# Latent attention in three-pass fp32 on one core: positional queries projected for two heads at once, and stage-opening weights split one stage earlier

## The reference

```python
def mla_layer(x, norm_g, w_in, q_norm, w_uq, w_out, k_nope, k_rope, v, cos, sin):
    h = rms_norm(x, norm_g)
    u = h @ w_in
    c_q = rms_norm(u[..., :Q_RANK], q_norm)          # 384 latents
    gate = u[..., Q_RANK:]                           # 8 heads x 128
    q = jnp.einsum("bsc,chd->bshd", c_q, w_uq)       # 128 + 64 per head
    q_nope = q[..., :QK_NOPE]
    q_rope = apply_rope(q[..., QK_NOPE:], cos[None, :, None], sin[None, :, None])
    o = causal_block_attention(q_nope, q_rope, k_nope, k_rope, v)
    y = o.reshape(bsz, seq, N_HEADS * V_DIM) * jax.nn.silu(gate)
    return y @ w_out
```

## Time and profile before

| what | value |
|---|---|
| median of 3 runs | 2606.91 us (2606.51 to 2610.33) |
| profiled execution | 2605.84 us |
| its span | 2604.0 us |
| mean granted TensorE clock | 0.980 |
| latent heads, 600 to 870 us | PE busy 263.3 of 270 us, DVE 150.9, ACT 121.5 |

### The profile page before, as it was taken

The page is one execution under the profiler, slowest core; times in us unless marked ns, Lnnn a source line. Parts: engine busy times, 40 slices in busy tenths (PEclk is TensorE's granted clock), DMA queues, the critical chain, the costliest instruction groups (busy, mean ns, idle before and its releaser), DMA issues. The chain is left out here.

```text
span 2604.0 us, 32719 instructions
## 1 busy us (share of the span) xinstructions
PE 2470.3 (95%) x12285; PEld 2046.1 (79%) x12285; DVE 1605.4 (62%) x2886; ACT 1197.0 (46%) x2167; POOL 191.5 (7%) x114
## 2 busy tenths in 40 slices
PE   7999899989999999899999999999899998999987
PEld 5777687877888777788888888888678786888876
DVE  6676766335655547666666666652666665888874
ACT  4554533224444444455555654432445434555542
POOL 0000021000000043000000000000122120000012
PEclk9999999999999999999999999999899999999998
DMA  3222321222221331111111011233344421111133
GB/s 132 81 75 87 126 89 57 73 88 82 65 92 55 114 109 57 41 41 41 34 41 41 26 40 41 97 129 139 130 153 144 132 81 37 41 32 48 49 118 113
DMA packets 89688, 206.56 MB, mean 79 GB/s; under 512 B 7120, under 2 KB 39760, under 8 KB 88528
## 3 DMA queue, kind: packets, MB, share of 16 engines
q1 hardware_dynamic: 89552, 204.72, 24.0%
HBM read 163.73 MB, written 40.96 MB: 79 GB/s over the span
## 5 line engine op out<-in xcount | busy, mean ns | idle before, releaser
L197 PE MATMUL acc<-operand_hi,w_hi 128*128 128x512 f32 x1878 | 762.0, 406 | 44.1 <-DVE w_lo L192 19.9
L199 PE MATMUL acc<-operand_hi,w_lo 128*128 128x512 f32 x1878 | 740.4, 394 | 0.0
L198 PE MATMUL acc<-operand_lo,w_hi 128*128 128x512 f32 x1878 | 739.5, 394 | 0.0
L197 PEld LDWEIGHTS acc<-operand_hi,w_hi 128*128 128x128 f32 x1878 | 357.3, 190 | 124.4 <-DVE w_lo L192 22.0
L199 PEld LDWEIGHTS acc<-operand_hi,w_lo 128*128 128x128 f32 x1878 | 356.5, 190 | 77.8
L198 PEld LDWEIGHTS acc<-operand_lo,w_hi 128*128 128x128 f32 x1878 | 357.4, 190 | 71.2 <-issue 3.6
L192 DVE TENSOR_TENSOR w_lo<-w_raw,w_hi 128x1024 fp32r<-128x1024 f32 (+1 forms) x209 | 234.6, 1123 | 187.1 <-ACT w_hi L186 185.4
L186 ACT ACTIVATE w_hi<-w_raw 128x1024 fp32r<-128x1024 f32 (+1 forms) x209 | 202.4, 969 | 287.0 <-PE aux L199 155.4
L197 PE MATMUL aux<-operand_hi,w_hi 128*128 128x512 f32 x602 | 246.8, 410 | 23.8 <-DVE w_lo L192 9.0
L199 PE MATMUL aux<-operand_hi,w_lo 128*128 128x512 f32 x602 | 237.9, 395 | 0.0
L198 PE MATMUL aux<-operand_lo,w_hi 128*128 128x512 f32 x602 | 237.8, 395 | 0.0
(11 more groups left out here) (424 smaller groups left out, 4175.6 us busy)
## 6 DMA issues: line engine op xcount, KB each, us to landing
w_raw<-in_stream SPq DMA_DIRECT2D x209, 512.0 KB, 3.6
ssd_e<-cs_scratch SPq DMA_DIRECT2D x8, 1024.0 KB, 7.3
g_scratch<-ssd_work SPq DMA_DIRECT2D x12, 512.0 KB, 2.9
ssd_xbc<-g_scratch SPq DMA_DIRECT2D x8, 768.0 KB, 5.5
y_scratch<-rnn_y SPq DMA_DIRECT2D x10, 512.0 KB, 2.6
out_a_raw<-y_scratch SPq DMA_DIRECT2D x20, 256.0 KB, 4.3
resid<-in_x SPq DMA_DIRECT2D x8, 512.0 KB, 8.4
g_scratch<-mlai_g SPq DMA_DIRECT2D x8, 512.0 KB, 2.9
```

The costliest lines, as they stand in the source:

```text
L197: pe.matmul(out, w_hi, x_hi, start=first, stop=False)
L198: pe.matmul(out, w_hi, x_lo, start=False, stop=False)
L199: return pe.matmul(out, w_lo, x_hi, start=False, stop=last)
```

## The change

1. The r tile now carries the 64 columns of two heads (b and b + 1, b even) side by side, without the swapped copy. It is loaded by two DMAs of 64-column pieces (`load_positional`). Odd heads have no r unit; a list `tiles` gives the order. ACT copies the product to SBUF (`evacuate("r")`), and DVE rotates a head in four operations, one step apart; for even heads b the next head is rotated at t = 1 to 4, for odd ones at t = 2 to 5, in front of the maximum except the first. `rope_low` moves to t = 6, behind `lower("k")`; ACT's `rotated` to t = 5. In odd heads q moves to t = 4.
2. Tile 2 of `out_b` and `out_sw` is split in step 7 of the last head or pair (`begun.split = 1`). The third tile of the layers behind `out_b` and `out_ssd` is split at the end of the projection in front, ahead of `final(1)`; `out_a` had that already.
3. `lag` = 2 for all: the second of the two tiles at the end runs two chunks behind the first.
4. For tile 0 of a projection DVE adds the residual behind the split.
5. In `mla_inputs` the third tile uses another PSUM bank; the second-last gate tile begins alone for three chunks; the v tile of head 0 is split to 256 columns only; the loads of tiles 2 and 3 of the heads are issued ahead of the last store of a gate.
6. The window attention takes the values out ahead of the keys.

```diff
 def project_halves(...):
+    skip = begun.split if begun is not None else 0
...
-        lag = 2 if after == "latent" else 0
+        lag = 2
...
-            if q + 2 < tiles + ahead:
+            if skip <= q and q + 2 < tiles + ahead:
...
+        if after != "end":
             split_hi(act, k, tile(tiles + 2))
...
-            dve.tensor_tensor(resid(q), total(q), resid(q), ALU.add).then_inc(k.acc_free[t.slot], 1)
-            if q + 2 < tiles + ahead:
+            if q and q + 2 < tiles + ahead:
+                dve.tensor_tensor(resid(q), total(q), resid(q), ALU.add).then_inc(k.acc_free[t.slot], 1)
+            if skip <= q and q + 2 < tiles + ahead:
                 split_lo(dve, k, tile(q + 2))
                 if extra and q + 2 < tiles:
                     piece_low(dve, q + 2)
+            if not q or q + 2 >= tiles + ahead:
+                dve.tensor_tensor(resid(q), total(q), resid(q), ALU.add).then_inc(k.acc_free[t.slot], 1)
...
-        if after == "latent":
+        if after != "end":
             split_lo(dve, k, tile(tiles + 2))
 def mla_inputs(...):
-        return k.acc[:, tile(h).slot, :]
+        return k.aux[:, 0, :] if h == 2 else k.acc[:, tile(h).slot, :]
...
-        store(count - 1)
...
+        front = 3
+        wait_tile(pe, k, tile(count - 2))
+        for n in range(front):
+            part(count - 2, n)
+        wait_tile(pe, k, tile(count - 1))
+        for n in range(front):
+            part(count - 1, n)
+        for n in range(front, DT):
+            for h in (count - 2, count - 1):
+                part(h, n)
...
-                split_lo(dve, k, tile(h + 2))
+                split_lo(dve, k, tile(h + 2), (KV_KT if h + 2 == count else DT) * P)
...
+def load_positional(sp, k, t, row):
+    sp.wait_ge(k.w_lo[t.slot], t.before)
+    for n, done in ((0, k.positional), (1, k.w_loaded[t.slot])):
+        sp.dma_start(k.w_raw[:, t.slot, 0:Q_KT * P].rearrange("p (t c) -> p t c", c=P)[:, :, HD * n:HD * n + HD],
+                     k.stream[row + 4 * n].rearrange("p (t c) -> p t c", c=P)[:, 0:Q_KT, 0:HD]).then_inc(done, 16)
 def mla_heads(...):
+    tiles = [(name, b) for b in range(MLA_HEADS) for name in (MLA_ORDER if b % 2 == 0 else "vqk")]
...
         for n in range(2, 4):
             load(n)
+        store_last(sp)
...
-                if t == 2 and more:
+                if t == 2 and more and b % 2:
                     units("r", b + 1)
-                if t == 3 and more:
+                if t == 3 + b % 2 and more:
                     units("q", b + 1)
...
+            if part < 2:
+                to, of = (at + 32 * m for m in (part, 1 - part))
+                dve.tensor_tensor(turned[to:to + 32, :], raw[of:of + 32, :], rope[64 + 32 * part:96 + 32 * part, :],
+                                  ALU.mult).then_inc(s["ra"], 1)
+            elif part == 2:
+                dve.wait_ge(s["ra"], 3 * b + 2)
+                dve.tensor_tensor(raw[at:at + 64, :], raw[at:at + 64, :], rope[0:64, :], ALU.mult).then_inc(s["ra"], 1)
+            else:
+                dve.wait_ge(s["ra"], 3 * b + 3)
+                dve.tensor_tensor(turned[at:at + 64, :], turned[at:at + 64, :], raw[at:at + 64, :], ALU.add
+                                  ).then_inc(s["rb"], 1)
...
-                        rotate(b + 1)
                         split("k", b + 1)
+                    if (3 <= t <= 5 and odd) or (1 <= t <= 4 and not odd):
+                        rotate(b + 1, t - 1 - odd)
                     if t == 6:
                         lower("k", b + 1)
+                        rope_low(b + 1)
...
+                    if t == 2 and odd:
+                        rotate(b + 1, 0)
-                        rope_low(b + 1)
 def window_attention(...):
+        t = Tile(j0, 1, per, 0)
+        act.wait_ge(k.tile_done[t.slot], t.before + 1)
+        act.activation(vt[:, :], k.acc[:, t.slot, :], ACT.Identity, bias=bv).then_inc(k.acc_free[t.slot], 1)
         t = Tile(j0, 0, per, 0)
...
+                    if n == 7:
+                        split_lo(dve, k, begun.tile(2))
```

More of the change, by code:

```diff
@@ L1275, in _ @@
         for h in range(2, count - 2):
-            wait_tile(pe, k, tile(h))
+            if h == 2:
+                pe.wait_ge(k.w_lo[tile(h).slot], tile(h).before + 1)
+            else:
+                wait_tile(pe, k, tile(h))
             multiply(pe, k, tile(h), acc(h), DT).then_inc(k.tile_done[tile(h).slot], 1)
@@ L1287, in _, with part @@
                 stats_pe_spread(pe, k, s, 1, k.aux[:, 1, :])
[L1288 to L1300, removed]
-                mm.then_inc(s["free"], 1)
+        def part(h, n):
+            t, w = tile(h), slice(order[n] * P, (order[n] + 1) * P)
+            for b in range(2):
+                mm = three_passes(pe, bank(acc(h), b), k.w_hi_sb[:, t.slot, w], k.w_lo_sb[:, t.slot, w],
+                                  bank(k.xh[:, order[n], :], b), bank(k.xl[:, order[n], :], b), n == 0, n == DT - 1)
+            if n == DT - 1:
+                mm.then_inc(k.tile_done[t.slot], 1)
+            if n < len(places) and h == count - 1:
+                mm.then_inc(s["free"], 1)
+        front = 3
[8 more added lines that the diff above has]
+                part(h, n)
     @block.gpsimd
@@ L1426, in mla_heads @@
     y = g
[L1427 removed]
+    t12 = sb("t12", [P, 2, S])
     v = sb("v", [P, S])
@@ L1478, in _ @@
             if b < last:
-                for n in range(4 * b + 6, 4 * b + 10):
+                for n in range(start(b + 1) + 2, start(b + 2) + 2):
                     load(n)
@@ L1629, in split @@
         def split(name, b):
+            if name == "r" and b < MLA_HEADS:
+                act.wait_ge(k.positional, 8 * b + 16)
             split_hi(act, k, tile(name, b), width(name, b))
@@ L1638, in evacuate @@
                 act.activation(kh[par], proj("k", b), ACT.Copy).then_inc(s["kh"], 1)
+            elif name == "r":
+                if b:
+                    act.wait_ge(s["rb"], b)
+                act.activation(t12[:, 1, :], proj("r", b), ACT.Copy).then_inc(k.acc_free[t.slot], 1)
             else:
@@ L1654, in _ @@
         evacuate("v", 0)
-        act.wait_ge(k.tile_done[tile("r", 0).slot], tile("r", 0).before + 1)
+        evacuate("r", 0)
         split("k", 0)
@@ L1684, in _ @@
                                    ACT.Copy).then_inc(s["pth"], 1)
+                if not more and t == 7:
+                    act.wait_ge(k.tile_done[begun.tile(0).slot], begun.tile(0).before + 1)
+                    split_hi(act, k, begun.tile(2))
                 if t == 0:
@@ L1698, in _ @@
                         evacuate("k", b + 1)
-                        split("r", b + 2)
+                        split("q" if odd else "r", b + 2)
                     if t == 7:
@@ L1758, in _ @@
         split("k", 0)
-        rotate(0)
+        for part in range(4):
+            rotate(0, part)
         lower("q", 0)
@@ L1763, in _ @@
         lower("k", 0)
-        split("r", 1)
+        split("q", 1)
         maximum(0, 0)
@@ L3181, in _ @@
                                bias=bk[rows(e), :]).then_inc(s[name], 1)
-        split_hi(act, k, Tile(j0, 2, per, 0))
         act_slopes(act, 0, 0)
-        t = Tile(j0, 1, per, 0)
-        act.wait_ge(k.tile_done[t.slot], t.before + 1)
-        act.activation(vt[:, :], k.acc[:, t.slot, :], ACT.Identity, bias=bv).then_inc(k.acc_free[t.slot], 1)
         split_hi(act, k, Tile(j0, 3, per, 0))
```

83 lines of the change are left out of this document (51 added, 32 removed).

## The result

The changed kernel took a median of 2594.43 us (2592.61 to 2595.43, four runs), the kernel before, beside it, 2608.36 us; the ratio is 0.995, 95% interval 0.9938 to 0.9963, so 9.7 to 16.2 us less. The profiled execution took 2594.74 us, 11.1 us less than that of before. Faster, as forecast, and within 2 us of the predicted 2592.7. The gain that was forecast is 14.2 us; the medians give 13.9, the two profiled executions 11.1.

A forecast was written before the change was run, and what follows sets the result against it. The prediction took PE, busy 95% of the span, as the bound nearly everywhere. Its terms summed to -14.2 us, which from the median of 2606.9 us gave 2592.7 us, with a range of 2580 to 2602 us.

The forecast's parts named there:

- four r units: Heads 1, 3, 5 and 7 lose their positional unit of 18 matmuls, 4.10 us each: -16.4 us.
- low queries behind keys: At seven changes of head, one more DVE operation ahead of the output makes PE wait 1.2 us more: +8.4 us.
- gate pair: Last two gate tiles, near 546 us: PE's 3.9 us gap and 2.4 us of half clock go, -6.3 us.
- opening of head 0: Narrow v split and earlier q load shorten the chain to the first score: -2.9 us, bounds 0 and -5.
- barrier at 428: PE no longer waits for ACT's copy out of the bank, since the new bank is free: -1.1 us.
- end of `out_b`: The split ahead of DVE's scalings delays ACT and PE at the barrier: +2.9 us; good-side bound -3.0.
- `out_ssd` and window start: Values turned earlier, but PE's next tile waits for the keys' bank; with clock and residual, +1.6 us.
- positional loads: Loads of 64 columns, in 256-byte pieces, have some 20 us before use: 0 us.
- rival D: Clock falls within the heads, 11 stretches of 2.4 us: 2619 us, slower than before; chance 0.04.
- B: Rival: new waits at head changes and the end of `out_b` don't come: 2581.4 us; chance 0.2.
- C: Rival: DVE becomes the bound in heads without an r unit, up to 8 us: 2600.7 us; chance 0.17.
- E: Rival: shared r tile is late or saves nothing, 16.4 us given back: 2609 us, no change; chance 0.04.

The follow-up runs named there:

- run 1: Changed kernel with the low part of the next head's queries moved to step 5, behind the maximum: 2580.72 us, ratio 0.9897.
- run 5: Changed kernel with the last two gate tiles beginning together again: 2593.5 us, ratio 0.9957.
- run 8: Kernel before with only the change's parts on the heads, the opening of head 0 and the bank at 428: 2597.27 us, ratio 0.9968.
- run 7: Changed kernel with tile 0's residual added ahead of the split again in `out_a` and `out_ssd`: one run, 2597.1 us.
- 9: Changed kernel with run 1's and run 7's edits, `out_b` scalings ahead of the split, first window query tile in a free bank: 2568.75 us, ratio 0.9853.
- 10: The version of run 9 without the lag of two chunks behind the differential attention and state-space stage: 2570.81 us, ratio 0.9853.

## Why the prediction was right, point by point

| step | predicted | measured | from |
|---|---|---|---|
| four r units | -16.4 | -19.0 | heads, before against run 1 |
| low queries behind keys | +8.4 | +12.3 | heads, after against run 1 |
| gate pair | -6.3 | -6.4 (3.9 pause, 2.5 clock) | profiles before and after; -5.5 in run 5 |
| opening of head 0 | -2.9 | -3.1 | 1.4 ahead of v, 1.7 up to the score |
| barrier at 428 | -1.1 | -1.1 | table |
| starts of `out_b`, `out_sw` | -0.7 | -1.2 | table |
| end of `out_b` | +2.9 | +2.2 pause, +2.5 inside | table |
| `out_ssd` and window start | +1.6 | +3.3, not shown to be the change | table; run 8 has it too |
| `out_a` | +0.3 | not to be told from 0 | run 7 |
| positional loads | 0 | 0 | below |

**The sum was better than its terms.** Two large ones missed. *The low queries*: the mechanism and its seven times were right (9.3 us against 8.4), but I priced the wait by its length and left its clock to rival D; that was 3 us more in the profile of the changed kernel, 1.3 of it behind the last change of head, where it came in every execution, and 1.7 where it came in some. *The r units*: the heads without the new wait are 19.0 us shorter, not 16.4. A pair of heads takes 76.55 us instead of 81.27, so 4.7 per unit removed. 4.1 is its 18 matmuls. The other 0.6 is not in the even head, which has lost the unit and is 3.9 us shorter, but in the odd one, which is 0.9 shorter: there two short waits of PE, 0.23 us for the probabilities and 0.15 for the output, are gone. In the kernel before they stood in nearly every head, in run 1 in every second one. The odd heads are those in which q stands a step later, but no run moves q alone, so that this is the reason is not shown. The two misses, +3.9 and -2.6, nearly cancel, and that is luck. So is part of the close hit of the whole: the two profiled executions differ by 11.1 us, not by 14.2, and only the medians by 13.9.

**Gate pair.** All of the gap went and full clock stands where 0.52 stood. The price of the slow part, 2.4 us, was right for the profile of before (2.5) and high for run 5 (1.6): it is not the same in each execution.

**Opening of head 0.** The number was right, the way to it only in part. Ahead of the v tile a wait of 1.2 us for its split is gone. Between the v tile and the first score the pauses of PE did not shrink: above the pace of 0.23 us for a matmul they add up to 5.7 us before and 5.9 after, with one of 4.1 us idle ahead of the score, as forecast (4.4). The 1.7 us there are the nine slow matmuls that stood behind the wait for q (3.75 us instead of 2.04) and are gone. The forecast had no clock in this term.

**Ends.** The chain behind `out_b` came out as stepped through: split, scalings, ACT, PE, 8.48 us after the start of the last matmul. The sign that I gave for it said about 8, while the times of my own chain say 1054.4 - 1045.2 = 9.2; the result lies between. The +2.5 inside the projection were not in the sum beyond the 0.8 for the lag: 0.9 are the lag, 1.0 a clock of 0.86 at its start, which came and went between executions, and the other 0.6 is open. In front of the window attention the bank of the keys took over from the split, as said; but the whole +3.3 is there without the change too (run 8), so the size of this term is neither borne out nor refuted.

**The rivals.** B (no new waits) fell with the 11.1 us. C (DVE the bound in odd heads) fell: run 1, with the same four rotations, has no wait for a maximum that the kernel before had not. D came true at a tenth of its price. (Its eighth stretch would bring 8 x 2.4 = 19.2 us and 2611.9, not 19.5 and over 2612, so it would have decided from the ninth.) My sign for it, a clock under 1.00 between 600 and 870 us, was a poor one: that stretch is at 0.99 before, after at 0.99, and 1.00 in run 1; only windows of 15 us around the changes of head show it. E fell: the loads of positional columns, in the part of the page on DMA issues for 650 to 700 us:

```profile
w_raw<-in_stream SPq DMA_DIRECT2D x2, 96.0 KB, 2.1
```

2.1 us for 96 KB in pieces of 256 bytes. They had landed by 682.3 us, and ACT split them at 698.9, so 17 us were to spare; I had said 20.

## What to carry to other kernels

An operation that goes into a hand-ordered queue is priced by its place, not by its length: 1.2 us in front of the output that PE waits for cost 12 us over seven changes of head (9 of waiting, 3 of clock), the same 1.2 us one step earlier, where DVE waited for ACT anyway, cost nothing. Before a wait is put into a queue, move ahead of it all that doesn't need it; this alone turned the early split behind `out_b` from a loss of 2.2 us into a gain of 1.0. And where a wait is removed, look up what holds the bank and not only who fills the operand: the first window tile stayed where it was until it had a bank of its own, and then 8.6 us went.

## What the runs showed of the hardware that I had not expected

**The same pause costs clock in some executions only.** In the nine profiled executions with the new waits, the clock fell behind the last one (2.1 us) every time, and behind the six of 1.5 us once in six of the executions and never in three. Which of the six it was changed between two executions of the same program (second and third pair of heads 80.89 and 79.97 us in one, 79.17 and 81.69 in the other). Each fall began 0.1 to 2.0 us after PE had started again and cost 1.3 to 1.7 us. Behind the waits of 0.8 us and less that stand in their place in runs 1, 9 and 10 it never fell. The start of `out_b` is at 0.86 or 1.00 in the same way, for 1.0 us. What decides it is open. Such steps would account for much of the spread of 5 us and more among the runs of one kernel; only one execution of each has a profile, so that isn't shown. They are why edits of 3 us had to be read in their own stretch, and they move these stretches too, by 1 to 2 us.

**Rows don't matter to DVE here.** A product of 1024 columns took 1.22 us on 32, on 64 and on 128 rows, so each of the two products on 32 rows in the new rotation is as dear as one on all rows.
